# Eight sample rows of an input projection as float32 column strips instead of a fifth token tile

## The chip, the cores and the metric

The kernel runs on one core of one Trainium2 chip. The metric is the device time of one launch in microseconds (us).

## The reference, cut to what matters

The program is one inference step of a two-layer decoder trunk, for 512 prompt tokens and 8 sample rows with shared weights. The first layer begins with one combined projection of the normalised rows to 4608 columns:

```python
hp, hs = rms_norm(yp, rms_mix_g[0]), rms_norm(ys, rms_mix_g[0])   # 512 x 1024, 8 x 1024
proj = h @ w_in                                                   # 1024 x 4608, once for hp, once for hs
rq, rk, rv, rg, dq, dk, dv = jnp.split(proj, EVEN_SPLITS, axis=-1)
```

Out of these parts come a retention (queries, keys, values, gate) and a differential attention. For each of the 8 samples the attention also reads 32 pages of 128 cached keys and values, 256 KB each, 128 MiB in all. After it come the output projection, a squared-ReLU MLP, and a second layer (gMLP and MLP). All is float32.

## The kernel before, in words

A float32 product is made as three products of split operands (fp32r): high times high, high times low and low times high. Weights come in chunks of 512 rows by 256 columns. SyncE loads chunk c into one of two raw buffers (`chunk_in`, L548), ScalarE writes its high part into one of four slots (`hi`, L505), VectorE or, for chunks 3 to 12, GpSimd its low part (`lo`, L513). In the input projection a macro m (of 18) is 256 columns: chunks 2m and 2m+1. TensorE does its five tiles of tokens one after another (`natural`, L1536): t = 0 to 3 with 128 tokens each, t = 4 (NT) with the 8 sample rows, 24 matmuls a tile, into the two PSUM banks NAT in turn. ScalarE takes each tile out of PSUM with the row's norm as scale (`evacuate`, L789).

All else in this stretch is hung on the slots (m, t) by `plan` (L110): each engine walks through the same list `AFTER[m, t]` in program order and does its part of the steps there. From slot (2, 4) on there are up to two cache steps per slot: a key step (VectorE multiplies two pages by the query and sums, L1220 and L1223) and, twenty steps later, value steps (TensorE, four column strips of 8 rows, L1579). Key pages have four buffers, value quads two. SyncE loads key pages, GpSimd value pages, each in its own list's order. Macros 6 to 9 also have the pairs of the differential attention (product L1648, maximum L1302, exponent L893, mix L1311, transposition, product L1664), macros 11 to 18 the retention. The transpositions of rotated heads (`turn`, L1507) go through one bank, TURN, in slots 3 and 4 or 1 and 2.

SyncE's order at the start is: constants and x, chunks 0 to 4, the store of x_kept (a copy of the transposed rows, L575), first keys, then the slots:

```python
for c in range(AHEAD + 2):                  # AHEAD = 3
    in_chunk(c)
sp.wait_ge(pro_copied, 2)
...
sp.dma_start(x_kept, xT[:, :, :]).then_inc(x_saved, 16)
```

Keys 2 and 3 and all of GpSimd's value pages wait for x_saved, since their buffers lie over xT. GpSimd's first split (chunk 3, L657) stands behind its first eight value pages, and macro 1 waits for it. The loads of the retention states (L593) wait until the last macro is multiplied, since they lie over its operands.

Of the kernel before, what the change touches and what calls it, by code (L numbers as in the profile page):

```python
# [26 lines left out]
P = 128  # L27
# [256 lines left out]
def build(nc, x_prompt, x_sample, state_ret, cache_k, cache_v, page_table, rms_mix_g, rms_ffn_g, w_ffn_up, w_ffn_down,  # L284
# [3 lines left out]
    with ExitStack() as ctx:  # L288
# [76 lines left out]
        ptb = r("ptb", [1, NS * NPAGES], I32)  # L365
        r = Region(x_at, x_end)
# [26 lines left out]
        xgs = tiny[:, 426:490].rearrange("p (k s) -> p k s", k=KD)  # L393
# [60 lines left out]
        nat_ready, nat_read, acc_read = sem("nat_ready"), sem("nat_read"), sem("acc_read")  # L454
        sq_made, sq_summed = sem("sq_made"), sem("sq_summed")
# [19 lines left out]
        xs_scaled, xs_hi = sem("xs_scaled"), sem("xs_hi")  # L475
# [66 lines left out]
        def _(sp):  # L542
# [210 lines left out]
        def _(act):  # L753
# [17 lines left out]
            act.wait_ge(xs_scaled, 1)  # L771
            act.activation(xg_hi[:, :, SEQ:T], xgs, ACT.Copy).then_inc(xs_hi, 1)
# [15 lines left out]

            def evacuate(m, t):  # L789

                rows = slice(0, P) if t < NT else slice(0, NS)
                if t < NT:
                    act.wait_ge(nat_ready, NT * m + t + 1)
                else:
                    act.wait_ge(chunk_multiplied, 2 * m + 2)
                src = ps[rows, NAT[(5 * m + t) % 2], 0:CW]
# [31 lines left out]
                if m in ROPED[4:]:  # L828
# [4 lines left out]
                    last.then_inc(nat_read, 1)  # L833
                else:
                    act.activation(dst, src, func, scale=rstdN[rows, t:t + 1]).then_inc(nat_read, 1)

            def act_step(step):
                kind, i = step[0], step[1] if len(step) > 1 else None
                if kind == "ropeq":
                    n = ROPED.index(i)  # L840
                    act.wait_ge(nat_read, 5 * (i + 1))
# [200 lines left out]
            def v_step(i):  # L1042
                for mm in range(2):
# [5 lines left out]
                    for t in range(NT + 1):  # L1049
                        if t < NT:  # L1050
                            act.wait_ge(nat_ready, NT * mac + (NT * N_IN + t + 1))
# [37 lines left out]
        def _(dve):  # L1089
# [9 lines left out]
            for k in range(KD):  # L1099
# [72 lines left out]
            def rot_step(m, t):  # L1172
# [6 lines left out]
                dve.wait_ge(nat_read, 5 * m + t + 1)  # L1179
# [18 lines left out]
            def dve_step(step):  # L1198
# [58 lines left out]
                elif kind == "so":  # L1257
# [7 lines left out]
                    dve.wait_ge(nat_read, 5 * N_IN)  # L1265
# [587 lines left out]
```

## Time and profile before

| | us |
|---|---|
| median of 3 runs | 2008.68 (2006.4 to 2014.68) |
| the profiled execution | 2011.98, its span 2010.2 |
| TensorE busy | 1818.9 (90%) |
| VectorE busy | 1010.6 (50%) |
| ScalarE busy | 581.5 (29%) |
| GpSimd busy | 436.6 (22%) |
| DMA | 288.01 MB, mean 143 GB/s |

In the profile PE is TensorE's matmuls, PEld its weight loads, DVE VectorE, ACT ScalarE, POOL GpSimd, SP SyncE. L12 is line 12 of the kernel. Busy shares over the whole span mix stages with different limits; the input projection is roughly the first 640 us. A timeline row has the start, the time from there to the end of what it merges, the engine, line, operation, and output<-inputs with their shapes; in brackets stands the idle time before it and what ended it.

### The profile page before, as it was taken

What the parts mean: (1) busy time and instruction counts of PE and PEld (TensorE: products, weight loads), DVE (VectorE), ACT (ScalarE), POOL (GpSimd) and SP (SyncE); (2) the same over time, 40 slices, a digit from 0 to 9 for tenths busy, and PEclk for the clock granted to TensorE, in tenths of its full rate; (3) what the DMA queues carried; (4) which work ended last, traced back from release to release, by engine and by line L of the source; (5) the groups of instructions that cost most, each with busy time, mean ns of one, the idle gap of its engine ahead of it and who ended that gap; (6) DMA issues with size and microseconds to landing.
All of it is one profiled execution on the core that took longest, in us unless ns stands there. A gap on an engine that the chain in (4) does not pass through costs nothing.

```text
span 2010.2 us, 35554 instructions
## 1 busy us (share of the span) xinstructions
PE 1818.9 (90%) x14155; PEld 1664.5 (83%) x14155; DVE 1010.6 (50%) x1312; ACT 581.5 (29%) x912; POOL 436.6 (22%) x522
## 2 busy tenths in 40 slices
PE   4786888777888799999999999989999999999998
PEld 4674554555555499999999999979999999999997
DVE  2689877899994544322333433353323453323321
ACT  4231232323233132321222232343223332212311
POOL 1221221133333012410330100024214223102400
PEclk8797788888898699999999999989999999999999
DMA  7257775699997623242232222212323323223231
GB/s 226 69 157 237 244 248 194 205 351 357 365 370 254 215 85 95 83 124 87 85 104 95 66 64 83 65 44 78 102 85 94 96 84 102 90 93 95 84 98 60
DMA packets 202092, 288.01 MB, mean 143 GB/s; under 512 B 13041, under 2 KB 149954, under 8 KB 201682
## 3 DMA queue, kind: packets, MB, share of 16 engines
q1 hardware_dynamic: 178432, 214.75, 33.2%
q0 software_dynamic: 21168, 68.64, 10.1%
q10 hardware_dynamic: 2362, 2.83, 0.4%
q8 instruction: 89, 1.46, 0.3%
q14 instruction: 41, 0.34, 0.1%
HBM read 274.96 MB, written 11.21 MB: 142 GB/s over the span
## 4 chain that ended last, share of the span: by engine, by line
PE 75%; DVE 7%; issue 7%; DMA 6%; ACT 3%; POOLq 2%; POOL 1%; SPq 0%; ACTq 0%; DVEq 0%
PE ps L1734 18%; PE ps L1736 18%; PE ps L1735 18%; PE ps L1544 4%; PE ps L1546 4%; PE ps L1545 4%; DMA vbuf<-in_cache_v 4%; PE ps L1579 2%; DVE kbuf L1220 2%; PE ps L1648 1%; POOLq L528 1%; DVE Sc L1223 1%; PE ps L1808 1%; PE ps L1507 1%; DMA xst<-in_x_prompt 1%
## 5 line engine op out<-in xcount | busy, mean ns | idle before, releaser
L518 DVE TENSOR_TENSOR w_lo<-raw,w_hi 128x1024 fp32r<-128x1024 f32 x238 | 327.3, 1382 | 456.9 <-ACT w_hi L511 455.8
L1734 PE MATMUL ps<-xg_hi,w_hi 128*128 128x260 f32 x1408 | 397.9, 283 | 1.0 <-DVE vn L1482 1.0
L1736 PE MATMUL ps<-xg_hi,w_lo 128*128 128x260 f32 x1408 | 397.8, 283 | 0.0
L1735 PE MATMUL ps<-xg_lo,w_hi 128*128 128x260 f32 x1408 | 396.6, 282 | 0.0
L511 ACT ACTIVATE w_hi<-raw 128x1024 fp32r<-128x1024 f32 x248 | 259.0, 1053 | 413.4 <-PE ps L1736 394.8
L1544 PE MATMUL ps<-w_hi,xg_hi 128*128 128x256 f32 (+1 forms) x1200 | 362.2, 302 | 12.6 <-DVE w_lo L518 6.1
L1545 PE MATMUL ps<-w_lo,xg_hi 128*128 128x256 f32 (+1 forms) x1200 | 352.8, 294 | 0.0
L1546 PE MATMUL ps<-w_hi,xg_lo 128*128 128x256 f32 (+1 forms) x1200 | 352.0, 293 | 0.0
L1736 PE MATMUL ps<-h_hi,w_lo 128*128 128x260 f32 x1024 | 289.3, 283 | 0.0
L1734 PE MATMUL ps<-h_hi,w_hi 128*128 128x260 f32 x1024 | 289.0, 282 | 0.0
L1735 PE MATMUL ps<-h_lo,w_hi 128*128 128x260 f32 x1024 | 288.3, 282 | 0.0
L1544 PEld LDWEIGHTS ps<-w_hi,xg_hi 128*128 128x128 f32 (+1 forms) x1200 | 218.0, 182 | 62.1 <-issue 39.1
L1734 PEld LDWEIGHTS ps<-xg_hi,w_hi 128*128 128x128 f32 x1408 | 265.0, 188 | 1.3 <-DVE vn L1482 1.2
L1736 PEld LDWEIGHTS ps<-xg_hi,w_lo 128*128 128x128 f32 x1408 | 265.0, 188 | 0.0
L1735 PEld LDWEIGHTS ps<-xg_lo,w_hi 128*128 128x128 f32 x1408 | 264.8, 188 | 0.1
L1545 PEld LDWEIGHTS ps<-w_lo,xg_hi 128*128 128x128 f32 (+1 forms) x1200 | 218.1, 182 | 8.0
L1546 PEld LDWEIGHTS ps<-w_hi,xg_lo 128*128 128x128 f32 (+1 forms) x1200 | 217.3, 181 | 8.2
L529 POOL DMA_DIRECT2D vbuf<-in_cache_v x256 | 138.0, 539 | 322.2 <-issue 185.6
L1736 PEld LDWEIGHTS ps<-h_hi,w_lo 128*128 128x128 f32 x1024 | 192.7, 188 | 0.0
L1734 PEld LDWEIGHTS ps<-h_hi,w_hi 128*128 128x128 f32 x1024 | 192.7, 188 | 0.0
L1735 PEld LDWEIGHTS ps<-h_lo,w_hi 128*128 128x128 f32 x1024 | 192.5, 188 | 0.0
L1220 DVE TENSOR_TENSOR kbuf<-kbuf,Qb 128x1024 f32<-128x1024 f32 x128 | 157.9, 1234 | 6.0 <-DMA kbuf<-in_cache_k 5.5
(278 smaller groups left out, 2471.8 us busy)
## 6 DMA issues: line engine op xcount, KB each, us to landing
kbuf<-in_cache_k SPq DMA_DIRECT2D x256, 256.0 KB, 4.3
vbuf<-in_cache_v POOLq DMA_DIRECT2D x256, 256.0 KB, 4.8
raw<-in_w_ffn_up SPq DMA_DIRECT2D x64, 512.0 KB, 3.8
raw<-in_w_ffn_down SPq DMA_DIRECT2D x64, 512.0 KB, 3.6
raw<-in_w_in_odd SPq DMA_DIRECT2D x48, 512.0 KB, 3.7
raw<-in_w_in_even SPq DMA_DIRECT2D x36, 512.0 KB, 6.2
raw<-in_w_out_odd SPq DMA_DIRECT2D x24, 512.0 KB, 3.4
raw<-in_w_out_even SPq DMA_DIRECT2D x12, 512.0 KB, 4.5
```

Of the source, the lines that this page charges most:

```text
L511: act.activation(w_hi[:, c.slot], raw[:, c.slot % 2], ACT.Copy).then_inc(hi_made, 1)
L518: dve.tensor_tensor(w_lo[:, c.slot], raw[:, c.slot % 2], w_hi[:, c.slot].bitcast(F32), ALU.subtract).then_inc(lo_made, 1)
L528: pg = eng.value_load(ptb[0:1, n:n + 1])
L529: eng.dma_start(dst, cache[0][bass.ds(pg, 1)].rearrange("a t h d -> (a t) (h d)")).then_inc(done, 16)
L1220: dve.tensor_tensor(kk[:, :, :], kk[:, :, :], Qb[:, s % 2, :].unsqueeze(1).broadcast_to([P, PER, 512]), ALU.mult).then_inc(k_weighed, 1)
L1544: pe.matmul(out, xh, wh, start=kk == 0, stop=False, skip_group_check=True)
L1545: pe.matmul(out, xh, wl, start=False, stop=False, skip_group_check=True)
L1546: mm = pe.matmul(out, xl, wh, start=False, stop=kk == KD - 1, skip_group_check=True)
L1579: last = pe.matmul(ps[at:at + 8, PV[s % 2], :], Pe[:, s % 2, QUAD * n + j, :], vbuf[i % Q_SLOTS][:, j, :], start=n == 0, stop=n == SQ - 1, ...
L1734: pe.matmul(out, wh, xh, start=kk == 0, stop=False, skip_group_check=True)
L1735: pe.matmul(out, wh, xl, start=False, stop=False, skip_group_check=True)
L1736: mm_ = pe.matmul(out, wl, xh, start=False, stop=kk == KC * groups - 1, skip_group_check=True)
```

## The change

The sample rows leave `natural`, which in the input projection now has four tiles (it counts `chunk_multiplied` at its last tile). Instead TensorE multiplies the scaled sample rows `xgs` (float32, not split) by the raw, landed chunk: `strips(c)` issues four float32 products with 8 stationary columns, one for each 128 of the chunk's 512 rows, each into its own 32 PSUM partitions, in the upper half of bank NAT[1]; two chunks accumulate. ScalarE copies the 128 x 256 result to SBUF (`strips_out`), and `fold_samples` adds the four strips by a product with the constant fold, into the upper half of NAT[0]. Strips of macro m+1 stand in front of tile (m, 3), the fold of macro m in front of tile (m, 2), and its evacuation behind that of tile 2. Tile (m, 1) waits for the copy. A raw buffer may only be loaded again when its strips are done, so `chunk_in` waits for `strip_made` too, and SyncE asks for chunk 2m+4 at t = 3 instead of t = 2. `clear_strips` writes zeros once over the strips' columns. The high and low parts of the samples' rows are no longer made for this projection. Waits on `nat_read` count four tiles a macro, and `sam_read` counts the samples' evacuations; the hunks with only such counts are left out below.

```diff
@@ -363,6 +363,8 @@
         ptb = r("ptb", [1, NS * NPAGES], I32)
+        part = r("part", [P, CW])
+        xgs = r("xgs", [P, KD, NS])[:, :, :]
         r = Region(x_at, x_end)
@@ -390,7 +392,6 @@
         rr = tiny[:, 320:340]
-        xgs = tiny[:, 426:490].rearrange("p (k s) -> p k s", k=KD)
         mxm, nmx, zz = (tiny[:, 340 + 2 * i:342 + 2 * i] for i in range(3))
...
@@ -548,6 +550,8 @@
                 wait(sp, lo_made, c.n - 1)
+                if isinstance(c.n, int) and c.n < 2 * N_IN + 2:
+                    wait(sp, strip_made, c.n - 1)
                 rows = w.rearrange("(g k p) n -> g p k n", k=KC, p=P)[g]
@@ -582,7 +586,7 @@
                 for t in range(NT + 1):
-                    if m > 0 and t == 2:
+                    if m > 0 and t == 3:
                         in_chunk(2 * m + AHEAD + 1)
@@ -768,8 +772,6 @@
                     act.activation(xT[:, k, 0:SEQ], ps[:, k % 4, :], ACT.Copy).then_inc(xT_act, 1)
-            act.wait_ge(xs_scaled, 1)
-            act.activation(xg_hi[:, :, SEQ:T], xgs, ACT.Copy).then_inc(xs_hi, 1)
             for c in range(2):
@@ -786,14 +788,23 @@
             act.activation(lamv[:, 2:4], lamv[:, 0:2], ACT.Exp).then_inc(lam_exps, 1)
+            def strips_out(m):
+
+                act.wait_ge(strip_made, 2 * m + 2)
+                wait(act, fold_ready, m)
+                act.activation(part[:, :], ps[:, NAT[1], CW:2 * CW], ACT.Copy).then_inc(part_copied, 1)
+
             def evacuate(m, t):
                 rows = slice(0, P) if t < NT else slice(0, NS)
-                if t < NT:
-                    act.wait_ge(nat_ready, NT * m + t + 1)
+                if t == NT:
+                    act.wait_ge(fold_ready, m + 1)
+                elif t == NT - 1:
+                    act.wait_ge(chunk_multiplied, 2 * m + 2)
                 else:
-                    act.wait_ge(chunk_multiplied, 2 * m + 2)
-                src = ps[rows, NAT[(5 * m + t) % 2], 0:CW]
+                    act.wait_ge(nat_ready, (NT - 1) * m + t + 1)
+                src = ps[rows, NAT[t % 2], 0:CW] if t < NT else ps[rows, NAT[0], CW:2 * CW]
+                read = nat_read if t < NT else sam_read
                 func = ACT.Copy
                 if m in ROPED:
                     i = ROPED.index(m)
...
@@ -958,12 +970,18 @@
             act.wait_ge(rstd_made, 1)
+            strips_out(0)
             for m in range(N_IN + 1):
...
                     if m < N_IN:
-                        evacuate(m, t)
+                        if t < NT:
+                            evacuate(m, t)
+                        if t == 2:
+                            evacuate(m, NT)
+                        if t == 3 and m + 1 < N_IN:
+                            strips_out(m + 1)
                         if t == 1:
...
@@ -1102,9 +1120,6 @@
                     dve.wait_ge(xT_act, k // 2 + 1)
-                if k == KD - 1:
-                    dve.wait_ge(xs_hi, 1)
-                    dve.tensor_tensor(xg_lo[:, :, SEQ:T], xgs, xg_hi[:, :, SEQ:T].bitcast(F32), ALU.subtract)
                 dve.scalar_tensor_tensor(xg_lo[:, k, 0:SEQ], ps[:, k % 4, :], column(GAIN[0], 0, k),
...
@@ -1525,15 +1543,35 @@
                     last = turn(ps[:, k % 4, P * t:P * t + P], xst[:, t, P * k:P * k + P], P)
                 last.then_inc(pro_turned, 1)
+            zero = Sc[0:NS].rearrange("p b n c -> p (b n c)")[:, 0:512]
+
+            def clear_strips():
+
+                pe.wait_ge(pro_set, 3)
+                pe.matmul(ps[:, NAT[1], CW:2 * CW], ones[0:NS, :], zero[:, 0:CW], start=True, stop=True, skip_group_check=True)
+
             def clear_sums():
-                pe.wait_ge(pro_set, 3)
-                zero = Sc[0:NS].rearrange("p b n c -> p (b n c)")[:, 0:512]
                 for bank in PV:
                     last = pe.matmul(ps[:, bank, :], ones[0:NS, :], zero, start=True, stop=True)
                 last.then_inc(pv_zeroed, 1)
-            def natural(m_chunks, t, bank):
+            def strips(c):
+
+                pe.wait_ge(raw_loaded[c % 2], Chunk(0, 0, 0, c).landed)
+                for j in range(KC):
+                    at = P // KC * j
+                    last = pe.matmul(ps[at:at + NS, NAT[1], CW:2 * CW], xgs[:, KC * (c % 2) + j, :], raw[:, c % 2, j, :],
+                                     start=c % 2 == 0, stop=c % 2 == 1, skip_group_check=True)
+                last.then_inc(strip_made, 1)
+
+            def fold_samples(m):
+
+                pe.wait_ge(part_copied, m + 1)
+                pe.matmul(ps[0:NS, NAT[0], CW:2 * CW], C["fold"], part[:, :], start=True, stop=True, skip_group_check=True
+                          ).then_inc(fold_ready, 1)
+
+            def natural(m_chunks, t, bank, last=NT):
                 tok = slice(P * t, P * t + (P if t < NT else NS))
                 out = ps[0:P if t < NT else NS, bank, 0:CW]
@@ -1544,9 +1582,9 @@
                         mm = pe.matmul(out, xl, wh, start=False, stop=kk == KD - 1, skip_group_check=True)
-                    if t == NT:
+                    if t == last:
                         mm.then_inc(chunk_multiplied, 1)
-                if t < NT:
+                if t < last:
                     mm.then_inc(nat_ready, 1)
...
@@ -1695,14 +1733,28 @@
                 for t in range(NT + 1):
                     if m < N_IN:
                         if t == 0:
-                            pe.wait_ge(lo_made, 2 * m + 2)
                             if m == 0:
                                 pe.wait_ge(xg_lo_made, KD)
                                 pe.wait_ge(xT_dve, KD // 2)
+                                pe.wait_ge(xs_scaled, 1)
+                                clear_strips()
+                                strips(0)
+                                strips(1)
+                            pe.wait_ge(lo_made, 2 * m + 2)
+                            wait(pe, sam_read, m)
                             if m == 1:
                                 clear_sums()
-                        wait(pe, nat_read, 5 * m + t - 1)
-                        natural([Chunk(0, 0, 0, 2 * m + g) for g in range(2)], t, NAT[(5 * m + t) % 2])
+                        if t < NT:
+                            wait(pe, nat_read, NT * m + t - 1)
+                        if t == 1:
+                            pe.wait_ge(part_copied, m + 1)
+                        if t == 3 and m + 1 < N_IN:
+                            strips(2 * m + 2)
+                            strips(2 * m + 3)
+                        if t == 2:
+                            fold_samples(m)
+                        if t < NT:
+                            natural([Chunk(0, 0, 0, 2 * m + g) for g in range(2)], t, NAT[t % 2], NT - 1)
                     for step in AFTER[m, t]:
                         pe_step(step)
```

## Rows read from the trace of the kernel before

**Rows 1.** The page's first line.
```profile
span 2010.2 us, 35554 instructions
```
**Rows 2.** Busy times by stretch: PE, PEld, DVE, ACT, POOL, clock, DMA share, GB/s.
```profile
58.00:180.00 122.00, 89.51 (x648) 80.72 (x647) 105.31 (x150) 35.19 (x58) 21.63 (x9) 0.82 0.39 119
180.00:420.00 240.00, 190.85 (x1075) 129.19 (x1072) 201.33 (x324) 65.91 (x181) 52.94 (x99) 0.81 0.73 241
420.00:606.00 186.00, 152.79 (x1069) 107.67 (x1068) 174.48 (x205) 56.45 (x97) 64.59 (x119) 0.93 1.01 365
606.00:642.00 36.00, 32.89 (x241) 24.14 (x240) 12.64 (x27) 13.76 (x23) 14.48 (x28) 0.95 0.70 217
642.00:666.00 24.00, 11.90 (x62) 4.02 (x62) 8.43 (x22) 5.96 (x12) 5.39 (x10) 0.58 1.04 353
700.00:1300.00 600.00, 595.91 (x4970) 588.23 (x4969) 220.22 (x250) 165.55 (x221) 99.50 (x86) 0.99 0.28 87
```
**Rows 3.** The chain of waits, in order of time: start, length, what.
```profile
31.66 0.37 SPq L552
32.15 8.86 DMA x_kept<-xT
...
52.10 2.36 POOL w_lo L518
54.50 3.77 PE ps L1533 x4
```
**Rows 4.** Timeline of PE, 447 to 452 us.
```profile
447.60 0.60 PE L1680 MATMUL ps<-rv,rkn 128*128 128x256 f32 x2
448.13 1.04 PE L1579 MATMUL ps<-vbuf,Pe 128*8 128x512 f32 x8
449.11 0.28 PE L1544 MATMUL ps<-w_hi,xg_hi 128*8 128x256 f32 x1
...
451.86 0.59 PE L1689 MATMUL ps<-rv,scm 128*128 128x256 f32 x2
```
**Rows 5.** Waits in 180 to 420: total us, times, longest.
```profile
DVE tiny L1302 <- PE ps L1650: 23.3, 12, 4.2
...
PE ps L1507 <- DVE pq L1311: 11.3, 7, 2.5
```
**Rows 6.** Timelines of PE and DVE, 101 to 110 us.
```profile
101.03 0.36 PE L1544 MATMUL ps<-w_hi,xg_hi 128*8 128x256 f32 x1
...
103.84 0.60 PE L1507 MATMUL ps<-cst,stg 128*128 128x128 f32 x4
...
109.01 1.49 DVE L1133 TENSOR_REDUCE tiny<-swp 128x20 f32<-128x1280 f32 x1 [5.62 <-ACT swp L843]
```
**Rows 7.** Tile raw in 420 to 620, and one issue from SP's timeline.
```profile
DMA to landing us min/median/max: 4.7/7.0/9.6
...
441.40 0.42 SPq L552 DMA_DIRECT2D raw<-in_w_in_even  x1
```
**Rows 8.** Timeline of SP.
```profile
642.03 11.16 SPq L593 DMA_DIRECT2D s0b<-in_state_ret  x8
```
**Rows 9.** Timeline of PE: first matmuls of tiles (0,0) to (0,3).
```profile
24.38 0.58 PE L1544 MATMUL ps<-w_hi,xg_hi 128*128 128x256 f32 x1 [6.15 <-DVE w_lo L518]
...
29.04 0.28 PE L1544 MATMUL ps<-w_hi,xg_hi 128*128 128x256 f32 x1
...
32.31 0.38 PE L1544 MATMUL ps<-w_hi,xg_hi 128*128 128x256 f32 x1 [0.28 <-ACT stg L835]
...
35.26 0.28 PE L1544 MATMUL ps<-w_hi,xg_hi 128*128 128x256 f32 x1
```
**Rows 10.** Timeline of ACT: its first evacuations.
```profile
31.80 0.82 ACT L835 ACTIVATE stg<-ps,small 128x256 f32<-128x256 f32 x2
```
**Rows 11.** Timeline of PE, 614 to 616 us.
```profile
614.51 1.12 PE L1579 MATMUL ps<-vbuf,Pe 128*8 128x512 f32 x8 [2.79 <-DMA vbuf<-in_cache_v]
615.56 0.58 PE L1544 MATMUL ps<-w_hi,xg_hi 128*128 128x256 f32 x1
```

More of the change, by code:

```diff
@@ L454, in build @@
         nat_ready, nat_read, acc_read = sem("nat_ready"), sem("nat_read"), sem("acc_read")
+        strip_made, part_copied, fold_ready, sam_read = (sem(n) for n in ("strip_made", "part_copied", "fold_ready", "sam_read"))
         sq_made, sq_summed = sem("sq_made"), sem("sq_summed")
@@ L474, in build @@
         s_roped, xT_act, xT_dve = sem("s_roped"), sem("xT_act"), sem("xT_dve")
-        xs_scaled, xs_hi = sem("xs_scaled"), sem("xs_hi")
+        xs_scaled = sem("xs_scaled")
         row_max, all_max, shifted, exped, o_copied, snew_rows = (
@@ L832, in evacuate @@
                         last = act.activation(dst[:, at], src[:, at], func, scale=dcy[rows, (m - 6) // 2, t, h:h + 1])
-                    last.then_inc(nat_read, 1)
+                    last.then_inc(read, 1)
                 else:
-                    act.activation(dst, src, func, scale=rstdN[rows, t:t + 1]).then_inc(nat_read, 1)
+                    act.activation(dst, src, func, scale=rstdN[rows, t:t + 1]).then_inc(read, 1)
             def act_step(step):
@@ L840, in act_step @@
                     n = ROPED.index(i)
-                    act.wait_ge(nat_read, 5 * (i + 1))
+                    act.wait_ge(nat_read, NT * (i + 1))
+                    act.wait_ge(sam_read, i + 1)
                     wait(act, roped, n)
@@ L1050, in v_step @@
                         if t < NT:
-                            act.wait_ge(nat_ready, NT * mac + (NT * N_IN + t + 1))
+                            act.wait_ge(nat_ready, NT * mac + ((NT - 1) * N_IN + t + 1))
                         else:
@@ L1178, in rot_step @@
                 xt, st4 = x.rearrange(two, a=2, c=d2), st.rearrange(two, a=2, c=d2)
-                dve.wait_ge(nat_read, 5 * m + t + 1)
+                if t < NT:
+                    dve.wait_ge(nat_read, NT * m + t + 1)
+                else:
+                    dve.wait_ge(sam_read, m + 1)
                 sn = sin.unsqueeze(1).broadcast_to([P, 2, d2])
@@ L1264, in dve_step @@
                     chain(dve.tensor_scalar(o4[:, :], o, mvo[:, 0:1], so4r, ALU.subtract, ALU.mult))
-                    dve.wait_ge(nat_read, 5 * N_IN)
+                    dve.wait_ge(sam_read, N_IN)
                     dve.tensor_tensor(o4[:, :], o4[:, :], srg4[:, :], ALU.mult).then_inc(so_done, 1)
@@ L1356, in dve_step @@
                     dve.wait_ge(r_normed, NT * h + n + 1)
-                    dve.wait_ge(nat_read, 5 * (11 + 2 * h) + n + 1)
+                    dve.wait_ge(nat_read, NT * (11 + 2 * h) + n + 1)
                     dve.tensor_tensor(out, out, sg[:, n, :], ALU.mult).then_inc(r_done, 1)
@@ L1442, in v_step @@
                     for t in range(NT + 1):
-                        dve.wait_ge(nat_read, 5 * mac + (5 * N_IN + t + 1))
+                        dve.wait_ge(nat_read, 5 * mac + (NT * N_IN + t + 1))
                         rows = slice(0, P) if t < NT else slice(0, NS)
@@ L1590, in pe_step @@
                     pe.wait_ge(turn_read, len(TURN_FILL))
-                    pe.wait_ge(nat_read, 5 * N_IN)
+                    pe.wait_ge(sam_read, N_IN)
                     for h in range(H):
@@ L1677, in pe_step @@
                     wait(pe, r_state, c)
-                    pe.wait_ge(nat_read, 5 * (10 + 2 * h) + NT)
+                    pe.wait_ge(nat_read, NT * (10 + 2 * h) + NT)
                     pe.matmul(ps[:, PAIR[0], 0:P], rkT[:, h, P * n:P * n + P], rqT[:, h, P * n:P * n + P], start=True, stop=True)
@@ L1778, in v_step @@
                         else:
-                            pe.wait_ge(nat_read, 5 * mac + (5 * N_IN - 5 + t + 1))
+                            pe.wait_ge(nat_read, 5 * mac + (NT * N_IN - 5 + t + 1))
                         natural(cs, t, t)
@@ L1797, in _ @@
             pe.wait_ge(R_copied, 1)
-            pe.wait_ge(nat_read, 5 * (N_IN + N_V))
+            pe.wait_ge(nat_read, NT * N_IN + 5 * N_V)
             for c in range(24):
```

1 line of the change is left out of this document (added).

## The prediction, on record before the result

> **What bounds the kernel now.** I read the page's first line, then the busy times by stretch, then the waits, then the chain of waits, and last single instructions in order of time. The profiled execution took 2011.98 us, span 2010.2 [rows 1]; the three timed runs have a median of 2008.68. The 1.8 us around the span stay, and I add the sum below to the median. The stretches [rows 2] show four regimes. From 700 us on TensorE is busy 596 of 600 us; the change issues nothing there. The input projection, from 58 to 642 us, is not TensorE's: VectorE is busy 105 of 122 us in 58 to 180, 201 of 240 in 180 to 420, 174 of 186 in 420 to 606, and in that last stretch the DMA engines are full as well (share 1.01, 365 GB/s), which is the cache pages at the memory's rate. Only in 606 to 642 is TensorE the full engine (33 of 36, DMA 0.70). In 642 to 666 the DMA engines are full again (1.04), with pages of values and the retention states. So what is worth asking of this change is not how many matmuls go, but which stretch had waited for them. The chain at the start [rows 3] has no fifth tile in it either: a weight load that SyncE issues at 31.66, the store of x_kept at 32.15 that lands 8.86 later, the value pages and a weight split on GpSimd, and at 54.50 the first product of macro 1.
>
> **What goes and what comes, on TensorE.** A fifth tile is 24 matmuls of 256 columns, from 449.11 to 451.86 [rows 4]: 2.75 us at the full clock (2.4 GHz). In its place stand, per macro: two groups of four strips, float32, 256 columns; a fold, float32, 128x256; a copy of 128x256 on ScalarE, about 0.47. The strips are not in the trace, but the value products are the same form at double width: four strips of 512 columns from 448.13 to 449.11, 0.98 us [rows 4]. If the cost goes with the columns a group is 0.49, if all of it were fixed 0.98. I take 0.5: the cost is the columns', since one float32 product of 512 columns alone takes half of the 3.77 at 54.50 [rows 3] at the half clock, 0.94 at the full one, and four take 0.98 side by side. The fold is nearest to the float32 product of 256 columns at 447.60, which gives 0.53. Sum per macro 1.5 (1.5 to 2.5), so 1.2 us less (0.25 to 1.25) of TensorE, 18 times: 22 us of work at most, twice that at the half clock.
> A rule speaks against it: TensorEngine Tiling (Array Packing) in the Trainium skill, section Key Properties, says that a change of tiling mode drains the array. The 0.98 holds one entry and one exit already, so the trace agrees or at least leaves room; by the rule a group would lie nearer the upper bound, and the saving nearer 0.25 a macro.
>
> **What that is worth, stretch by stretch.** In 58 to 420 VectorE leads. Its waits for TensorE in 180 to 420 are 23.3 us in 12 places, all before the maximum of the attention pairs (L1302) [rows 5]. Only three of these twelve stand in a slot that loses its tile (slots 6,4 to 8,4), so the gain there is at most 3 x 2.75 = 8; but three slots each get strips (1.0) and fold (0.5), and twice that at the half clock, which costs 4.5 to 9. TensorE itself waits 11.3 us for VectorE's mixed scores in the same loop [rows 5], so part of the tile's time is wait that stays. I take 0 (-5 to +5).
> From macro 2 to 3 VectorE sits idle 5.62 before 109.01 [rows 6], and TensorE is ahead of it in that chain. There the tile 101.03 to 103.84 goes (2.81), strips and fold come (1.5), and what the tile covered comes out: the second transposition must wait until ScalarE has copied the first out of the one bank (0.6 of copy, some 0.3 on either side, about 1.2, an estimate from the pitch of these rows). 0 (-1.3 to +1).
> In 420 to 606 the DMA engines are full; fewer matmuls move no bytes: 0 (-2 to +3). The loss side: chunk 2m+4 is now asked for one slot later, behind two more key steps, some 5 us, and lands after 7.0 (4.7 to 9.6) [rows 7]; ScalarE's split of it stood 12 us after its issue (441.40 [rows 7], 453.20) where tightest in this stretch. That just holds. SyncE now also waits there for strips on TensorE, and behind it stand the key pages, which have four buffers.
> At the end the loads of the retention states wait for the last chunk's multiplication. They went out at 642.03 [rows 8]. Now the last tile is t=3, so they go some 5 us earlier; but the stretch is bytes, and what the earlier start can use is only the idle share in 636 to 642 (0.86 busy: 0.8 us) and a value product that stands 2.75 earlier less its load's own wait. I take -1 (-3 to 0).
>
> **The start, where a wait is added on the path.** This is the term that decides. SyncE issues chunks 0 to 4 and then, in its own order, the store of x_kept. chunk_in now waits for strip_made c-1; for chunk 4 that is three groups of strips, and the third, strips(2), stands on TensorE in front of tile (0,3). Before, chunk 4 waited only for VectorE's split and went out at 31.66 [rows 3]. What does TensorE do until then? Tile (0,1) began at 29.04 [rows 9]; now it waits for part_copied, since the strips share its bank. ScalarE makes this copy ahead of its first evacuation, which it reached at 31.80 [rows 10]; the removed split of the samples' rows gives 0.3 of that back. So the copy runs 31.5 to 32.0, and tile (0,1) starts at 32.0, where before tile (0,2) stood (32.31). Then: tile (0,1) 2.85, fold 0.53, tile (0,2) 2.85, strips(2) 0.5: 38.75. A tile at the full clock is the 2.95 from 32.31 to 35.26 less a short wait. The load goes out at 38.8 instead of 31.66: 7.1 us late. x_kept is 0.5 behind it, as before. Behind x_kept wait: SyncE's keys 2 and 3, and GpSimd, which sends eight value pages and only then makes the split that macro 1 needs (52.10 to 54.50 [rows 3]). Nothing on that path is shortened, so the first product of macro 1 goes from 54.50 to 61.6.
> The clock can make it more. TensorE is idle between tile (0,0), done by 28.5 to 29.4, and 32.0. After an idle of 2.79 before 614.51 the first matmul at 615.56 took 0.58 instead of 0.28, which is the lower of the clock's two levels (1.2 GHz) [rows 11]. A tile at that level is the 4.66 from 24.38 to 29.04 [rows 9] (at the lower level but for its end), 1.9 more. So 7.1 to 9.0; I take 8.
> The Trainium skill has the same, TensorE: Matmul & The Clock Gate, section What's actually happening: an idle array falls back to half its rate. By that rule this term would be 9.0, by a clock that stays 7.1.
> The three matmul groups before tile (0,0) (a clearing product of 256 columns, a quarter of those 3.77 for two of 512, so 0.94, and two groups of strips at the half clock, 0.98 each) start at about 21.9 and end at 24.8; the tile began at 24.38. They cost nothing, since (0,1) waits for ScalarE anyhow.
> Is the late start made good later? From 109 on VectorE works without a gap that has to do with the clock on the wall; every load is asked for by a consumer. I see nothing that absorbs it.
>
> **Sum.** +8 (start), 0, 0, 0, -1 (end): +7, so 2008.7 + 7 = 2015.7 us. Against the profiled execution it is 2011.98 to about 2019. In percent +0.35: within the 0.5% (10 us) that a measurement of this kernel can tell from no change.
>
> **The rivals.**
> A. TensorE's saved time counts in the projection. For it: 606 to 642, and the 23.3 us of waits; if half of 22 us comes through in 58 to 606 and the start costs 7, the result is 2004.7; if all comes through and the clock gives twice in the slow places, 1990 to 1998. Against it: VectorE's share and the full DMA engines. 0.12 for a gain over 0.5%.
> B. Slower by more than 10 us, by one mechanism: SyncE stands at chunk 2m+4 until TensorE has reached (m,3), and the key pages behind it come late. In macro 8 chunk 20 went out at 297.4, two key steps on are about 307, and TensorE began tile (8,3) at 310.9, so SyncE would stand some 4 us; if VectorE runs dry by 2 us in each of five macros, +10 on top: 2026. It decides once a stall is longer than the pages in the four key buffers cover. 0.30 together with the upper end of the start term (9) and of the attention loop (+5).
> C. The start is not delayed, because some other wait there was as late: 2007.7. Against it: the chain has x_kept's store and its issue back to back with the load. 0.10, within the 0.5%.
> D. The strips don't run side by side: a group then costs four times 0.49, a macro 4.4 instead of 2.75, and TensorE's 1.7 a macro more add to B's case. Against it the 0.98 of four strips. It is inside B's chance.
> My forecast (2010 to 2018.7) has 0.48. So faster by over 0.5%: 0.12, within: 0.56, slower: 0.32. Range 2003 to 2024: below it A's strong form, above it B's.
>
> **What would show it.** Chunk 4's issue at 38 to 41 us, x_kept right behind it, and macro 1's first product at 61 to 64. Tile (0,1) waiting for ScalarE's copy. Strips of a chunk at 0.5 and a fold at 0.53, the fifth tile gone. The 420 to 606 stretch as long as before (186), with the DMA share at 1. States' loads some 5 us nearer to the last tile. Wrong if the first product of macro 1 stands at 55 to 58, or if the projection from there to its end is over 5 us shorter or longer than the 588 us from 54.50 to 642.03.

## The result and the profile after

The changed kernel takes 2036.1 us (median of four runs, 2027.8 to 2041.2) where the kernel before, on the same chip, takes 2011.2: ratio 1.0119, 95% interval 1.0096 to 1.0141. A second set gave 2037.5 us and 1.0141 (1.0113 to 1.0169). The mean of the two ratios, 1.013, makes the change about 26 us slower, where 7 were forecast. The first profile caught the fastest of its four runs (2027.8); the second, of the second set, with a span of 2035.5, is the more typical, so both are used.

The first lines of the two profiles, to stand beside [rows 1]:

```profile
span 2026.1 us, 35464 instructions
```
```profile
span 2035.5 us, 35464 instructions
```

Busy times by stretch in the first profile, columns as in [rows 2]:

```profile
180.00:420.00 240.00, 178.76 (x1008) 114.35 (x1008) 196.25 (x319) 66.74 (x187) 48.97 (x90) 0.82 0.70 228
420.00:606.00 186.00, 145.32 (x994) 99.62 (x994) 171.29 (x200) 54.38 (x99) 64.33 (x120) 0.86 1.00 356
...
700.00:1300.00 600.00, 588.92 (x4904) 579.77 (x4905) 227.10 (x269) 166.53 (x227) 99.55 (x86) 0.99 0.29 91
```

TensorE has 12 us less to do in 180 to 420, and nothing has become quicker: VectorE is busy 5 us less, the DMA engines move 228 GB/s instead of 241. In 420 to 606 the granted clock is 0.86 instead of 0.93.

Where the time goes is read best from one instruction that both kernels have, the first product of a tile. Here it is for tiles (1,0), (6,0), (11,0) and (17,3), in the kernel before, then in the two profiles of the changed one (the last column's form names the same product; only line numbers moved):

```profile
58.20 0.58 PE L1544 MATMUL ps<-w_hi,xg_hi 128*128 128x256 f32 x1
...
179.96 0.58 PE L1544 MATMUL ps<-w_hi,xg_hi 128*128 128x256 f32 x1
...
424.83 0.39 PE L1544 MATMUL ps<-w_hi,xg_hi 128*128 128x256 f32 x1
...
633.18 0.39 PE L1544 MATMUL ps<-w_hi,xg_hi 128*128 128x256 f32 x1
```
```profile
67.29 0.58 PE L1582 MATMUL ps<-w_hi,xg_hi 128*128 128x256 f32 x1
...
188.57 0.58 PE L1582 MATMUL ps<-w_hi,xg_hi 128*128 128x256 f32 x1
...
439.07 0.58 PE L1582 MATMUL ps<-w_hi,xg_hi 128*128 128x256 f32 x1
...
651.95 0.39 PE L1582 MATMUL ps<-w_hi,xg_hi 128*128 128x256 f32 x1
```
```profile
66.06 0.58 PE L1582 MATMUL ps<-w_hi,xg_hi 128*128 128x256 f32 x1
...
187.92 0.58 PE L1582 MATMUL ps<-w_hi,xg_hi 128*128 128x256 f32 x1
...
441.14 0.58 PE L1582 MATMUL ps<-w_hi,xg_hi 128*128 128x256 f32 x1
...
659.27 0.39 PE L1582 MATMUL ps<-w_hi,xg_hi 128*128 128x256 f32 x1
```

The differences to before are +9.1, +8.6, +14.2, +18.8 in the first profile and +7.9, +8.0, +16.3, +26.1 in the second. So three losses: 8 to 9 at the start, nothing up to macro 6, 6 to 8 in the attention loop (macros 6 to 10), 5 to 10 in macros 11 to 17. The third is the least certain: the profile of kernel 2 below, which changes nothing in macros 11 to 17, is 4.9 longer there than the same profile of before, so at most the excess over that, 0 to 5, is clearly the change's. From (17,3) to the end of the span 3 and 1 come back (15.9 and 25.3 are left).

**The start.** SyncE's issues in the first profile, which answer to the first two of [rows 3], and the chain's links to macro 1:

```profile
40.91 0.37 SPq L556 DMA_DIRECT2D raw<-in_w_in_even  x1
41.38 0.45 SPq L579 DMA_DIRECT2D x_kept<-xT  x1
```
```profile
41.38 8.78 DMA x_kept<-xT
...
61.18 2.36 POOL w_lo L520
63.58 3.78 PE ps L1556 x4
```

And on TensorE the start of tile (0,1), the fold, and the two groups of strips (macro 1's) ahead of (0,3):

```profile
32.08 0.38 PE L1582 MATMUL ps<-w_hi,xg_hi 128*128 128x256 f32 x1 [3.60 <-ACT part L795]
...
36.45 0.78 PE L1571 MATMUL ps<-part,cst 128*8 128x256 f32 x2
...
40.19 1.05 PE L1564 MATMUL ps<-raw,xgs 128*8 128x256 f32 x16
```

Tile (0,1) waits 3.60 us for ScalarE's copy. Its first product is still at the full clock (0.38); from about 33.5 on its products take 0.41 instead of 0.28, and the tile 4.37 (32.08 to 36.45) instead of the forecast 2.85. The strips of two chunks take 1.05, and when the first chunk's are done the load of chunk 4 goes out, at 40.91, which is 9.25 later than the 31.66 of before; x_kept goes out behind it, and the first product of macro 1 stands at 63.58 instead of 54.50. This is the step as it was forecast, at its upper bound.

**The attention loop.** Waits of VectorE and TensorE in 180 to 420, first profile; compare [rows 5]:

```profile
DVE tiny L1320 <- PE ps L1688: 27.7, 11, 5.4
...
PE ps L1525 <- DVE pq L1329: 18.2, 8, 4.2
```

VectorE's wait is 4.4 us longer and TensorE's 6.9, though TensorE has less to do. Slots (7,3) and (7,4) show how. First TensorE and VectorE in the kernel before:

```profile
255.09 0.49 PE L1650 MATMUL ps<-cst 128*128 128x128 f32 x2
...
261.57 0.38 PE L1507 MATMUL ps<-cst,pq 128*128 128x128 f32 x2
...
270.80 0.41 PE L1507 MATMUL ps<-cst,pq 128*128 128x128 f32 x2 [1.25 <-DVE pq L1311]
```
```profile
266.26 0.96 DVE L1302 TENSOR_REDUCE tiny<-ps 128x2 f32<-128x768 f32 x1 [1.89 <-PE ps L1650]
...
275.43 0.96 DVE L1302 TENSOR_REDUCE tiny<-ps 128x2 f32<-128x768 f32 x1 [0.87 <-PE ps L1650]
```

Then the same in the changed kernel:

```profile
264.73 0.49 PE L1688 MATMUL ps<-cst 128*128 128x128 f32 x2
...
267.73 1.90 PE L1564 MATMUL ps<-raw,xgs 128*8 128x256 f32 x16
...
273.76 0.38 PE L1525 MATMUL ps<-cst,pq 128*128 128x128 f32 x2
...
278.20 0.49 PE L1688 MATMUL ps<-cst 128*128 128x128 f32 x2
...
283.26 0.66 PE L1525 MATMUL ps<-cst,pq 128*128 128x128 f32 x2 [4.13 <-DVE pq L1329]
```
```profile
278.72 0.96 DVE L1320 TENSOR_REDUCE tiny<-ps 128x2 f32<-128x768 f32 x1 [5.44 <-PE ps L1688]
...
290.38 0.96 DVE L1320 TENSOR_REDUCE tiny<-ps 128x2 f32<-128x768 f32 x1 [3.36 <-PE ps L1688]
```

At (7,3) VectorE is idle for 5.44 instead of 1.89. The strips run at the half clock there: 1.90 for what took 1.05 at 40.19. From the last pair product of slot (7,2) to VectorE's maximum it is 13.99 (264.73 to 278.72), where it was 11.17 (255.09 to 266.26). Of these 2.8 us more the strips are 1.8, two small groups ahead of them at the half clock 0.8, and ScalarE's added copy 0.3; the tile itself takes as long as before, since it began at the half clock there too. The other 0.75 of VectorE's wait comes from its standing closer behind TensorE at the start of the slot: its maximum before began 0.52 after that pair product's start, where it had been 1.27. At (7,4), where the tile stood, TensorE now waits 4.13 instead of 1.25, its clock is down behind the wait, and VectorE's next wait is 3.36 instead of 0.87.

**Macros 11 to 17.** Chunk 26's load stood behind twelve issues of key pages in the kernel before (its issue, at 441.40, is in [rows 7]):

```profile
422.79 18.55 SPq L529 DMA_DIRECT2D kbuf<-in_cache_k  x12
```

In the changed kernel it stands behind sixteen. Here are SyncE's timeline and ScalarE's split of the chunk (the bracket: idle before it, and what ended that):

```profile
436.72 26.06 SPq L531 DMA_DIRECT2D kbuf<-in_cache_k  x16
462.88 0.39 SPq L556 DMA_DIRECT2D raw<-in_w_in_even  x1
```
```profile
470.10 1.06 ACT L513 ACTIVATE w_hi<-raw 128x1024 fp32r<-128x1024 f32 x1 [3.69 <-DMA raw<-in_w_in_even]
```

The load lands after 7.1, and ScalarE stands 3.69 for it. Against the start of tile (11,3) it goes out 5.7 later than before (3.5 behind it instead of 2.2 ahead). ScalarE has four such waits in 420 to 650, 12.4 us in all (five and 14.4 in the second profile); the kernel before has none.

### The profile page after: what moved, and what is told of

It is laid out like the page before. It is cut to its first block, busy times and chain, and to the rows that moved or that the text cites. A ratio compares the mean times of both kernels' runs of the same rounds, so it can differ in the third digit from the quotient of the medians.

```text
span 2026.1 us, 35464 instructions
## 1 busy us (share of the span) xinstructions
PE 1803.5 (89%) x14049; PEld 1636.1 (81%) x14049; DVE 1010.8 (50%) x1311; ACT 583.9 (29%) x928; POOL 435.8 (22%) x522
## 4 chain that ended last, share of the span: by engine, by line
PE 75%; DVE 8%; issue 6%; DMA 5%; ACT 3%; POOLq 1%; POOL 1%; SPq 0%; ACTq 0%; DVEq 0%
PE ps L1786 18%; PE ps L1788 18%; PE ps L1787 18%; PE ps L1582 4%; PE ps L1584 4%; PE ps L1583 4%; DMA vbuf<-in_cache_v 4%; PE ps L1617 2%; DVE kbuf L1238 2%; DVE Sc L1241 2%; POOLq L530 1%; PE ps L1686 1%; PE ps L1860 1%; PE ps L1525 1%; DMA xst<-in_x_prompt 1%
## 5 line engine op out<-in xcount | busy, mean ns | idle before, releaser
L1582 PE MATMUL ps<-w_hi,xg_hi 128*128 128x256 f32 (+1 forms) x1056 | 319.9, 303 | 7.8 <-DVE xg_lo L1414 4.1
L1583 PE MATMUL ps<-w_lo,xg_hi 128*128 128x256 f32 (+1 forms) x1056 | 310.1, 294 | 0.0
L1584 PE MATMUL ps<-w_hi,xg_lo 128*128 128x256 f32 (+1 forms) x1056 | 309.4, 293 | 0.0
L1582 PEld LDWEIGHTS ps<-w_hi,xg_hi 128*128 128x128 f32 (+1 forms) x1056 | 205.5, 195 | 51.6 <-issue 42.2
L1583 PEld LDWEIGHTS ps<-w_lo,xg_hi 128*128 128x128 f32 (+1 forms) x1056 | 204.9, 194 | 2.9
L1584 PEld LDWEIGHTS ps<-w_hi,xg_lo 128*128 128x128 f32 (+1 forms) x1056 | 204.2, 193 | 2.8
```

The lines of the kernel that those rows point to most:

```text
L1582: pe.matmul(out, xh, wh, start=kk == 0, stop=False, skip_group_check=True)
L1583: pe.matmul(out, xh, wl, start=False, stop=False, skip_group_check=True)
L1584: mm = pe.matmul(out, xl, wh, start=False, stop=kk == KD - 1, skip_group_check=True)
```

## The experiments

Times are medians; ratios are to the kernel before on the same chip, with their 95% intervals. Where two kernels are compared, it is by these ratios, since not all ran on the same chip. A per mille is 2 us. Kernel n is the kernel of experiment n. What is said of positions and waits comes from one profile of each kernel.

| kernel | us | ratio | interval |
|---|---|---|---|
| changed (second set) | 2037.5 | 1.0141 | 1.0113 to 1.0169 |
| changed, strips thinned | 2035.3 | 1.0120 | 1.0083 to 1.0157 |
| changed, x_kept first | 2021.7 | 1.0051 | 1.0030 to 1.0072 |
| the same, strips early | 2025.8 | 1.0076 | 1.0049 to 1.0102 |
| the same, filler in macros 6 to 10 | 2016.4 | 1.0034 | 1.0021 to 1.0046 |
| the same, filler in 6 to 16 | 2011.9 | 1.0008 | 0.9990 to 1.0025 |
| the same, strips thinned | 2009.2 | 0.9999 | 0.9983 to 1.0016 |
| before, fifth tile thinned | 2012.0 | 1.0008 | 0.9992 to 1.0025 |
| before, chunk load late | 2015.4 | 1.0038 | 1.0021 to 1.0056 |
| before, x_kept first | 2004.0 | 0.9970 | 0.9954 to 0.9986 |
| the same, chunk load late | 2010.1 | 0.9987 | 0.9972 to 1.0002 |
| before, x_kept first, filler | 2002.8 | 0.9961 | 0.9944 to 0.9978 |

**1. x_kept first, in the changed kernel.**

```
-            for c in range(AHEAD + 2):
+            for c in range(AHEAD + 1):
                 in_chunk(c)
...
             sp.dma_start(x_kept, xT[:, :, :]).then_inc(x_saved, 16)
+            in_chunk(AHEAD + 1)
```


> The changed kernel, but SyncE issues the store of x_kept before chunk 4, so it no longer stands behind chunk 4's wait for the strips. Theory S (the start is lost in SyncE's order alone: 9.1 us at the first product of macro 1): that product comes back to 55 or earlier (from 63.6), and the whole run is 8 to 17 us shorter than the changed kernel's 2036, that is 2019 to 2028. The delay of chunk 4 itself stays (issue near 40), which costs nothing if macro 2 waits for nothing of it. Rival (the start is lost in TensorE's own order, tile (0,1) behind ScalarE's copy and the strips): the product stays past 60, and at most 2 us are won.

Chunk 4 still goes out at 40.40, but x_kept at 27.08, and the chain reads:

```profile
27.08 10.41 DMA x_kept<-xT
...
48.97 2.36 POOL w_lo L520
51.38 3.77 PE ps L1557 x4
```

The first product of macro 1 is at 51.38 instead of 63.58, and the ratio falls by 8 per mille from the mean of the two sets, 16 us (by the intervals 10 to 21). What stood behind chunk 4 in SyncE's order cost the time; the late chunk itself cost next to nothing, since at tile (6,0) this kernel is only 1.3 behind kernel 2 below, which has the same order and an early chunk 4. The rival falls.

**2. The same edit in the kernel before.**

> Control: the kernel before with the same reordering of x_kept and chunk 4. Theory S: macro 1's first product waits for the chain x_kept, value pages, split; x_kept goes out when the transposed x is complete, a few us before 31.66, so the product comes up to 8 us earlier (46 to 54.5) and the run ends 0 to 8 us below the kernel before. If x_kept was not held by chunk 4 before, nothing moves (within 1 us).

The product comes 4.4 us earlier (50.11), the run ends 3.0 per mille (6 us, 3 to 9 by the interval) below before. So x_kept had been held there too, and of the 16 us above about 6 are an old loss and 10 the change's own start term. This is a version that beats both kernels.

**3. The changed kernel with thinned strips.** In `strips` one product of 8 columns instead of four of 256; the fold is 8 columns wide after macro 0.

> The changed kernel with all its waits and its order, but each chunk's strips cut to one product of 8 columns and, after macro 0, the fold to 8 columns: it leaves out nearly all of the samples' rows of the projection. Theory L (the 8 us lost between tile (6,0) and (8,0) are TensorE's time for strips and fold, at half clock, in the slots 2 and 3): tile (8,0) stands 8 to 10 us behind the kernel before instead of 16, and the run is 8 to 12 us below the changed kernel, 2024 to 2028. Rival B (SyncE's new wait for the strips makes pages or chunks late): the order is the same, so tile (8,0) stays at +15 to +17 and the run within 3 us of 2036. Rival A (all TensorE time counts): up to 18 x 1.5 x 1.0 to 2.0 = 27 to 54 us less.

2035.3: nothing gained that could be measured. My theory L, that the time of strips and fold is what the loop lost, falls at this run: tile (8,0) stands at +16.4 (+16.1 with full strips). So does rival A. Rival B's two numbers came true, but they hold for anything that stays when only work is taken out. At (7,4) VectorE waits as it did, and at (7,3) 1.1 less:

```profile
278.99 0.96 DVE L1320 TENSOR_REDUCE tiny<-ps 128x2 f32<-128x768 f32 x1 [4.33 <-PE ps L1689]
...
290.64 0.96 DVE L1320 TENSOR_REDUCE tiny<-ps 128x2 f32<-128x768 f32 x1 [3.37 <-PE ps L1689]
```

The granted clock in 180 to 420 is 0.77 (0.82 with the full strips). The less TensorE had to do, the slower it ran: tile (7,3) took 4.93 (269.10 to 274.03) where it took 4.21 with the strips ahead of it (269.55 to 273.76).

**4. The kernel before with a thinned fifth tile.** `natural` skips 21 of its 24 products for t = NT.

> The kernel before with the fifth tile of the input projection cut from 24 products to 3 (7 of 8 of the samples' rows' sum are left out), all waits, loads and copies kept: 2.4 us less of TensorE in each of 18 macros at the full clock, 43 us in all. It measures what the tile is worth by itself. Theory L: VectorE and the pages bound the projection, so nearly nothing comes out, 0 to 10 us (2000 to 2010). Rival A: half or more comes out, 1968 to 1990.

2012.0, ratio 1.0008: 21 of 24 products of 2.75 us, 18 times, are 43 us of TensorE's work at the full clock, and no time went with them that could be measured (by the interval -2 to +5 us). That is the worth of what the change set out to remove. The clock went down here too, 0.93 to 0.87 in 420 to 606, and the wait behind (7,4) is the 3.36 of the changed kernel; but the one before it is 1.63 (1.89 in the kernel before):

```profile
263.00 0.96 DVE L1302 TENSOR_REDUCE tiny<-ps 128x2 f32<-128x768 f32 x1 [1.63 <-PE ps L1655]
...
274.66 0.96 DVE L1302 TENSOR_REDUCE tiny<-ps 128x2 f32<-128x768 f32 x1 [3.36 <-PE ps L1655]
```

In this profile tile (7,0) stands at -3.6 and tile (8,0) at +0.4: what the thinned tiles had won up to there went again in macro 7.

**5. The changed kernel again.**

> The changed kernel unaltered, for a second profile and a time beside the others. The first profile was the fastest of its four executions (2027.8 of 2027.8 to 2041.2). Expected: 2030 to 2040, start term +9 again, the further loss over the first profile (about 8 us) either in the attention loop (180 to 420: theory clock) or in 420 to 640 (theory late chunks: ScalarE's splits waiting for the weight chunk, 12.4 us in 4 places in the first profile, none before).

2037.5; its profile is the second one above. Of the 9 us more than in the first, 3 fall in the attention loop, 5 in macros 11 to 17 and 2 behind them, and 1 less is lost up to macro 6; no one place has them alone.

**6. Strips of the even chunk early.** x_kept first; `strips(2 * m + 2)` ahead of tile (m,1), and SyncE's load of chunk 2m+4 back at t == 2. This kernel leaves the sums of the samples' rows incomplete, since tile (m,1) opens its own sum in the same bank between the two groups (this is read from the edit, not tested by itself).

> The changed kernel with the store of x_kept first and, besides, the strips of chunk 2m+2 in front of tile (m,1) instead of (m,3), so that SyncE can ask for chunk 2m+4 at t=2 again. Theory late chunks: the strips hold the landing buffer until TensorE reaches (m,3), so the next chunk is asked late and ScalarE's split waits for it (13 us in 4 places in 420 to 650). With the buffer free two tiles earlier these waits go, and the run is 4 to 10 us below the kernel with x_kept first alone (2021.7), that is 2012 to 2018. Theory clock (the idle TensorE falls to half rate and the pair products of the attention loop come late): the loop's step of 8 us between tile (7,0) and (8,0) stays, and the total changes by less than 3 us.

ScalarE's waits for the chunk are gone from the list, 13.0 us before, but the run is no faster (1.0076 against 1.0051, the intervals overlap), and tile (9,0) stands 4.8 later than with x_kept first alone in the profiles. The 4 to 10 us that the theory of the late chunks expected did not come, and over macros 11 to 17 this profile still loses 5.4 (7.2 with x_kept first alone), so by these two profiles ScalarE's waits for the chunk explain about 2 of that stretch's loss. The loop's step between tiles (7,0) and (8,0) stays, as the theory of the clock had it (7.4). Whether the strips in their new slot cost the loop what the load gave is not shown.

**7. A filler where the tile was, macros 6 to 10.** It takes away idle time and keeps every wait of the change (x_kept is first here too).

```
+                        if t == NT and 6 <= m < 11:
+                            wait(pe, nat_read, NT * m + NT - 1)
+                            for i in range(3 * KD):
+                                pe.matmul(ps[0:NS, NAT[0], 0:CW], xg_hi[:, i // 3, 0:NS], xg_hi[:, i // 3, 0:CW],
...
```


> The changed kernel with the store of x_kept first and 24 products of 256 columns, whose result nobody reads, in the slot (m,4) of macros 6 to 10, where the removed tile stood; it adds 14 to 28 us of TensorE work. Theory clock: the removed tile kept TensorE at the full clock through slot (m,4); with the filler the pair products after it take 0.91 instead of 1.65, VectorE's wait for them at slot (7,4) goes from 3.4 to 0.9, and tile (9,0) stands 3 to 6 us earlier against the kernel with x_kept first. Rival (the order and the waits of the strips cost it, not the clock): tile (9,0) stays within 2 us or comes later, by up to 5 x 1 us.

24 products more in each of five slots, 14 us at the full clock, and the run gets no slower for it; it is 1.7 per mille (3.4 us) faster, though the intervals overlap; by the profiles tile (9,0) stands at -5.0 instead of +7.4, twice the gain expected there, of which most is lost again by tile (17,0) (+8.6 against +13.5). The same pair products in slot (7,4), with x_kept first alone, then with the filler:

```profile
271.73 0.66 PE L1526 MATMUL ps<-cst,pq 128*128 128x128 f32 x2 [4.12 <-DVE pq L1330]
...
272.32 1.90 PE L1618 MATMUL ps<-vbuf,Pe 128*8 128x512 f32 x8
...
274.14 1.65 PE L1687 MATMUL ps<-kT,qT 64*128 64x384 f32 x2
```
```profile
266.64 0.41 PE L1526 MATMUL ps<-cst,pq 128*128 128x128 f32 x2 [1.30 <-DVE pq L1330]
...
266.98 1.04 PE L1618 MATMUL ps<-vbuf,Pe 128*8 128x512 f32 x8
...
268.65 0.91 PE L1687 MATMUL ps<-kT,qT 64*128 64x384 f32 x2 [0.62 <-ACT pq L906]
```

and VectorE's waits at (7,3) and (7,4) with the filler:

```profile
262.11 0.96 DVE L1321 TENSOR_REDUCE tiny<-ps 128x2 f32<-128x768 f32 x1 [5.45 <-PE ps L1689]
...
271.27 0.96 DVE L1321 TENSOR_REDUCE tiny<-ps 128x2 f32<-128x768 f32 x1 [0.87 <-PE ps L1689]
```

After a wait of 4.12 everything takes twice as long or nearly (1.90, 1.65); after 1.30 nothing does. The wait behind (7,4) is back to its 0.87, the number forecast. The 5.45 at (7,3), where the strips are, stays.

**8. The filler in macros 6 to 16.** It waits for `sam_read, m + 1` here.

> The changed kernel with the store of x_kept first and the unread 24 products in the slot (m,4) of macros 6 to 16, not 6 to 10 alone. With the filler in 6 to 10 the attention loop was back (tile (9,0) at -5.0 against the kernel before), but of that 13.6 us were lost again up to tile (17,0), where the granted clock was 0.87 (0.93 in the kernel before). Theory clock for that stretch too: with the filler there the clock comes back to 0.92 or more and tile (17,0) stands 5 us or more earlier, the run at 2008 to 2013. Rival (there the cache pages and the chunk asked for late bound it, the clock is only a sign of idle time): within 2 us of 2016.4, or later.

2011.9; against kernel 7 the clock in 420 to 606 comes back from 0.87 to 0.92, tile (17,0) stands at +3.4 instead of +8.6, and the ratio falls by 2.6 per mille more. ScalarE's waits for the chunk fall to 4.7 in 2 places. Against x_kept first alone, where the intervals lie apart, the whole filler wins 4.3 per mille (9 us, 3 to 14 by the intervals) with work that computes nothing.

**9. The same with thinned strips.**

> As the kernel with the filler in macros 6 to 16, and the strips cut to one product of 8 columns per chunk and the fold to 8 columns (it leaves out nearly all of the samples' rows). What is left of the change is its waits and SyncE's later slot. Theory (what strips and fold still cost is their time at TensorE in the loop's slots 2 and 3): 4 to 8 us less than with them. Rival (they cost nothing, the waits and the late chunk do): within 2 us of it.

2009.2, 0.9 per mille less, which the intervals cannot tell from nothing: strips and fold cost about 2 us of run time here, and anything from none to 7 is possible. That is nearer to the rival (within 2 us) than to the theory (4 to 8), and rules out neither.

**10. The late slot of the load alone, in the kernel before.**

```
-                    if m > 0 and t == 2:
+                    if m > 0 and t == 3:
                         in_chunk(2 * m + AHEAD + 1)
```


> The kernel before with one edit of the change alone: SyncE asks for chunk 2m+4 at t=3 instead of t=2, behind two more steps of key pages. Theory late chunks: part of the loss in 420 to 640 is this alone: 2 to 6 us slower than before, ScalarE's splits waiting for raw. Rival (it is the wait for the strips that makes them late, not the slot): no difference, within 2 us.

Slower by 3.8 per mille, 8 us (4 to 11), more than the 2 to 6 expected. Its profiled run was its fastest of ten (2006.8 of a median 2015.4) and shows little: in 420 to 650 ScalarE has 3.5 us of waits for the chunk, in two places, and VectorE waits 6.6 us for key pages (3.1 in the kernel before). That the later load costs time is shown by the times, the path only in part.

**11. The same with x_kept first.**

> The kernel before with the store of x_kept first, and SyncE's chunk 2m+4 asked for at t=3 instead of t=2; nothing else of the change. The changed kernel with x_kept first, the filler and the thinned strips stands at 2009.2, and the kernel before with x_kept first at 2004.0. Theory: those last 5 us are the later slot of the load in SyncE's order (6.4 us when it was moved alone), so this run gives 2007 to 2012, 1.0 to 1.5 per mille over or under the kernel before. Rival: the slot is not it and the waits for the strips are, so it stays within 2 us of 2004.

2010.1, as the theory had it; to kernel 2 the ratio is 1.7 per mille higher, 3.4 us, with intervals that overlap. VectorE's waits for key pages in 420 to 650 are 9.8 us here and 4.0 in kernel 2. The two estimates for the slot are 3 and 8 us, and what separated kernel 9 from kernel 2 (2.9 per mille, 6 us) lies between them; the waits for the strips need no share of their own, but aren't excluded.

**12. Filler in the kernel before.** x_kept first, and 8 unread products ahead of TensorE's wait for the mixed scores in the 16 units.

> The kernel before with the store of x_kept first, and 8 unread products of 256 columns (0.9 us at the full clock) ahead of TensorE's wait for the mixed scores in each of the 16 units of the attention loop. If the half clock after such waits costs VectorE its 4 us waits (units 11, 13, 15), the filler wins 3 to 6 us against 2004.0. Rival: 0.9 us each on a ring that is bound by its latency makes it 0 to 8 us slower.

2002.8, 0.9 per mille below kernel 2: not told apart from it, and short of the 3 us expected at least. The granted clock in 180 to 420 rose from 0.82 to 0.88, but VectorE's waits for the pair products hardly moved (22.8 us after 23.7). In the kernel before, whose tile keeps slot (m,4) filled, more filler brings nothing that can be measured, and a higher mean clock alone is no gain.

## Why the prediction was wrong

- **Start, +8 (7.1 to 9.0): right**, with mechanism and place: +9.1 and +7.9 at tile (1,0), and experiment 1 takes them away. It takes away more (16 us) because the same order held x_kept in the kernel before, which the chain in [rows 3] showed and I didn't price. One reading in it was loose: at the full clock a tile's first product takes 0.39 (424.83), not 0.28, so the 0.58 is to be held against that; it is the half clock all the same.
- **Prices: right at the full clock.** Strips of a macro took 1.17 and the fold 0.75 on the mean (21.1 and 13.5 us for 18 of each). At the full clock they took 1.05 and 0.60, against a forecast of 1.0 and 0.53, and at the half clock 1.9 and 1.02; three of the strips and six of the folds were wholly or mostly at the lower level.
- **Attention loop, 0 (-5 to +5): the step that failed first**, measured +5.6 and +8.3 from (6,0) to (11,0). The sum set a gain of up to 8 against 4.5 to 9 of strips and folds, and said that part of the tile's time "is wait that stays", priced at nothing. The gain was not there: with the tile thinned alone (experiment 4) the loop is 1.8 longer, not shorter. And the wait is not free for who comes after it. The 4.13 on TensorE before 283.26 brings the half clock, and the pair products behind it, for which VectorE waits, take 1.65 instead of 0.91 (both numbers are shown in experiment 7). The mechanism was in my own text, for the start ([rows 11]), and I didn't carry it to the slots that lose their tile. The Trainium skill's page TensorE: Matmul & The Clock Gate, section What's actually happening, has an idle array fall back to half its rate; the traces agree (1.90 and 1.04 for the same eight products). Experiment 8 gives the price, 9 us for the whole filler. The loop's length goes with VectorE's waits for the pair products in 180 to 420, kernel by kernel:

| kernel | those waits, us | loop, against before, us |
|---|---|---|
| before | 23.3 | 0 |
| 4 (tile thinned) | 25.8 | +1.8 |
| changed, two profiles | 27.7 and 28.7 | +5.6 and +8.3 |
| 1 (x_kept first) | 30.9 | +10.2 |
| 3 (strips thinned) | 31.0 | +11.2 |
| 6 (strips early) | 36.7 | +15.1 |
| 7, 8 and 9 (filler) | 20.3, 22.8, 24.0 | -0.5, +0.5, +2.9 |

- **420 to 606, 0 (-2 to +3): failed second**, +4.5 and +9.8 from (11,0) to (17,3), of which kernel 2 has 4.9 without the change. "That just holds" was the sentence. The margin was worked out from one chunk; with the load 5.7 later and behind sixteen issues of key pages instead of twelve, ScalarE stands 12 to 14 us for the chunks, and experiments 10 and 11 put the later slot at 3 to 8 us of run time.
- **Rival B** had the sign, but its stall did not do the harm. SyncE did stand for the strips of chunks 18, 20 and 22, in macros 7 to 9, by 2.5 to 2.8 us each (chunk 20: last key page issued by 324.58, the load at 327.41), where B had 4. Yet VectorE's waits for key pages in 180 to 420 were 2.3 and 4.8 us in the two profiles and 3.5 in the kernel before, so it did not run dry by 2 us in each of five macros. For chunk 26 SyncE did not wait for the strips at all: they were done at 459.4, the load went out at 462.88.
- **End, -1 (-3 to 0): right.** The states' loads go out at 655.10, 13.1 later than before while tile (17,3) is 18.8 later: 5.7 nearer, and 3 and 1 us come back.
- **The tile is worth nothing: right**, and stronger than I put it (experiment 4).
- **Range.** In ratios times 2010 the changed kernel is at +26. Taken in this order of edits, issuing x_kept first takes 16 of it, 6 of them the old loss, so 10 are the change's; the filler takes 9, thinned strips 2, and 6 are left to kernel 2, which fits the slot of the load (3 and 8 when measured alone). 10 + 9 + 2 + 6 = 27. My own upper ends (9, 5, 1, 3 and 0) add up to 18, and the range was cut at 15, though rival B, with 0.30, was itself priced at 2026, above its end. The two failed terms lay 1 to 7 beyond theirs.
- **Open.** A thinned tile alone (4) lowers the clock as well and costs nothing, while in the changed kernel the filler wins 9 us. At (7,3) the two differ by VectorE's wait, 5.44 and 1.63, which the strips, their place at the half clock and ScalarE's copy make up; but with the strips thinned (4.33) the loop is no shorter, so this is not the whole difference. The filler also shifts what comes after it in time, and that it works through the clock alone is the reading that fits these rows, not one that leaves nothing else. How the late load turns into run time is shown by the times, and in part by VectorE's waits for key pages (4.0 in kernel 2, 9.8 in kernel 11); the path between was not followed.

## What to carry to other kernels

Before you take work off an engine that waits anyway, ask what its idle time does to the work behind it: here 43 us less of TensorE's products bought nothing, and behind idle gaps of 4 us the products on the path took nearly twice as long. When an edit adds a wait to a queue, or moves a load in it, list what stands behind it and what now stands ahead, for every occurrence and not for one. And where a chain shows two issues back to back, with the later of them on the path, try the other order: swapping the two gave 6 us in the kernel before for one moved line.

## What was not expected

- Eight value products of four strips (128x512) take 1.04 us at the full clock and 1.90 after TensorE had waited 4.12; with a wait of 1.30 before it they took 1.04.
- Unread products made the kernel faster: eleven slots of 24 by 9 us (five slots by 3, within overlapping intervals).
- The same kernel's profile can differ by 9 us from its next (2026.1 and 2035.5), spread over two stretches; one profile of a changed kernel is not enough to size its terms.
